# Attention as a stream of heads, with split decays, in a hybrid decoder step on one Trainium2 core

## What is computed

```python
def stick_breaking(q, k, v, q_pos0, sb_bias):
    ...
        mask = k_pos[None, :] < q_pos[:, None]
        z = jnp.einsum('bqhd,bkhd->bhqk', qb, kb).astype(jnp.float32) * scale + bias
        log_1m = jnp.where(mask, jax.nn.log_sigmoid(-z), 0.0)
        log_w = jax.nn.log_sigmoid(z) + lax.cumsum(log_1m, axis=3, reverse=True) - log_1m
        w = jnp.where(mask, jnp.exp(log_w), 0.0)
        outs.append(jnp.einsum('bhqk,bkhd->bqhd', w.astype(vb.dtype), vb))
```

## Time and profile before

| | |
|---|---|
| three runs | 2433.86, 2426.59, 2428.55 us; median 2428.55 |
| the profiled execution | 2428.46 us, span 2426.8 us, granted clock 0.998 |
| PE busy | 2382.4 us (98%), PEld 2183.8 (90%) |
| DVE, ACT, POOL busy | 1241.0 (51%), 994.5 (41%), 114.9 (5%) |
| traffic | 417.10 MB in 122660 packets, 23387 of them under 512 B |

### The profile page before, as it was taken

The page is one execution under the profiler, slowest core; times in us unless marked ns, Lnnn a source line. Parts: engine busy times, 40 slices in busy tenths (PEclk is TensorE's granted clock), DMA queues, the critical chain, the costliest instruction groups (busy, mean ns, idle before and its releaser), DMA issues.

```text
span 2426.8 us, 43808 instructions
## 1 busy us (share of the span) xinstructions
PE 2382.4 (98%) x18802; PEld 2183.8 (90%) x18802; DVE 1241.0 (51%) x1725; ACT 994.5 (41%) x1399; POOL 114.9 (5%) x232
## 2 busy tenths in 40 slices
PE   6999999999999999999999999999999999999998
PEld 5999999965699999999999999887777999999998
DVE  5533246755576333357523347755554758633245
ACT  5422235635456222346422245533223546522243
POOL 0000000122100000000000000012222100000000
PEclk9999999999999999999999999999999999999999
DMA  8555345785537653565754255544545456642254
GB/s 308 180 183 183 124 149 179 252 211 139 190 113 228 215 173 95 188 206 175 261 184 156 83 168 189 188 153 165 170 165 165 136 177 182 206 126 88 87 179 155
DMA packets 122660, 417.10 MB, mean 172 GB/s; under 512 B 23387, under 2 KB 27611, under 8 KB 122211
## 3 DMA queue, kind: packets, MB, share of 16 engines
q1 hardware_dynamic: 88962, 301.92, 39.1%
q10 hardware_dynamic: 18144, 62.03, 7.1%
q0 software_dynamic: 15360, 50.34, 6.3%
HBM read 390.84 MB, written 23.41 MB: 171 GB/s over the span
## 4 chain that ended last, share of the span: by engine, by line
PE 88%; DVE 5%; ACT 3%; DMA 2%; issue 1%; SPq 0%; ACTq 0%; POOL 0%; DVEq 0%; POOLq 0%
PE PS L2026 70%; PE PS L1425 3%; PE PS L1960 2%; DVE WL L2318 2%; PE PS L1990 2%; PE PS L1355 1%; ACT WH L2140 1%; DMA AFIRST<-in_w_ada 1%; PE PS L791 1%; PE PS L1309 1%; PE PS L1340 1%; PE PS L1350 1%; PE PS L753 1%; DMA RAW<-in_w_out 1%; PE PS L1321 1%
## 5 line engine op out<-in xcount | busy, mean ns | idle before, releaser
L2318 DVE TENSOR_TENSOR WL<-RAW,WH 128x1024 fp32r<-128x1024 f32 (+1 forms) x478 | 633.0, 1325 | 647.9 <-ACT WH L2140 647.2
L2026 PE MATMUL PS<-HH,WH 128*128 128x260 f32 x3432 | 796.6, 285 | 3.2 <-DVE QKVS L1119 1.8
L2026 PE MATMUL PS<-HH,WL 128*128 128x260 f32 x3432 | 786.5, 283 | 0.0
L2026 PE MATMUL PS<-HL,WH 128*128 128x260 f32 x3368 | 769.6, 283 | 0.0
L2140 ACT ACTIVATE WH<-RAW 128x1024 fp32r<-128x1024 f32 (+1 forms) x478 | 542.2, 1135 | 425.4 <-PE PS L2026 267.0
L2026 PEld LDWEIGHTS PS<-HH,WH 128*128 128x128 f32 x3432 | 569.9, 188 | 25.4 <-issue 16.8
L2026 PEld LDWEIGHTS PS<-HH,WL 128*128 128x128 f32 x3432 | 569.4, 188 | 0.0
L2026 PEld LDWEIGHTS PS<-HL,WH 128*128 128x128 f32 x3368 | 557.0, 188 | 0.6 <-issue 0.2
L2026 PE MATMUL PS<-GH,WH 128*128 128x260 f32 x1408 | 386.4, 285 | 0.9 <-DVE WL L2318 0.8
L2026 PE MATMUL PS<-GL,WH 128*128 128x260 f32 x1408 | 384.2, 283 | 0.0
L2026 PE MATMUL PS<-GH,WL 128*128 128x260 f32 x1408 | 383.5, 283 | 0.0
(11 more groups left out here) (340 smaller groups left out, 2317.5 us busy)
## 6 DMA issues: line engine op xcount, KB each, us to landing
RAW<-in_w_in SPq DMA_DIRECT2D x236, 512.0 KB, 3.7
RAW<-in_w_out SPq DMA_DIRECT2D x120, 704.0 KB, 4.0
AW<-in_w_ada ACTq DMA_DIRECT2D x114, 512.0 KB, 5.5
RAW<-in_w_odd SPq DMA_DIRECT2D x60, 512.0 KB, 3.7
RAW<-in_w_odout SPq DMA_DIRECT2D x30, 512.0 KB, 3.9
RAW<-in_w_even SPq DMA_DIRECT2D x28, 512.0 KB, 4.0
KV<-in_v_pages POOLq DMA_DIRECT2D x32, 256.0 KB, 4.8
SR<-in_ret_past POOLq DMA_DIRECT2D x32, 256.0 KB, 4.0
```

The costliest lines, as they stand in the source:

```text
L2026: last = nc.tensor.matmul(ps[:, x, 0:HT], w[:, k * P:(k + 1) * P], src[k0 + k][:, x, :], start=(begin and t == 0), stop=(end and t == 2))
L2318: nc.vector.tensor_tensor(low_, RAW[:, from_:from_ + w], high_.bitcast(F32), ALU.subtract).then_inc(lo_done, 1)
```

## The change

- **The stream of heads.** The loop runs over single heads. In head h block i: `sums(h, i)`, then `scores(h+3, i)` alone, then for even h > 0 a quarter of `values(h/2 - 1)`, and in heads 0, 3, 5 and 7 a quarter of `values_past`. The scores of head 1 and `sums_past` move into units 26 and 27; those of head 2 stand between unit 27 and the loop.
- **Split decays.** The softplus of a head is split into an fp32r high part (`high_part`, ACT, L918) and low part (`low_part`, DVE, L1105), 1280 columns each, and the sums become 20 fp32r matmuls per head (L810) in place of ten float32 ones, with fp32r copies of the triangle and of ones.
- **|z|** is taken by DVE for heads 0 to 2 and by ACT for heads 3 to 7 (`decay`). `Z` has four places and the decays five; `log_weights` now writes into the decay's place.
- **Rows of 16.** The host pads `pool_past` to 16 values, `US` is loaded and stored as a whole, and the host drops the first value of each row. The small loads are reordered. DVE waits for these loads (`ev_in`) at unit 0 of `evin`, and for the four stores (`pool_out`) before it writes `Z` of head 1; ACT waits for the stores too, before `high_part(0)`.

The core of the diff:

```diff
+        ZQ = [at(n, [CAUSAL], o)[:] for n, o in zip(("ZA", "ZB", "ZC", "ZD"), (sq_at, up_at, low_at, free_at))]
+        HOME_OF = (0, 1, 2, 3, 4, 0, 2, 3)
...
+                    for dst, src in ((US[:], pool_past), (PT[0:1, :], table), (PWT[:], pool_w), (RCP[:], pool_r),
+                                     (PSC[:], pool_s), (BIAS[:], bias_b)):
...
-                                     (pool_p, UP[:, :, SEQ + 1:SEQ + 16]), (pool_n, US[:, :, :, 1:16])):
-                        sp.dma_start(dst, src).then_inc(out_done, 16)
+                                     (pool_p, UP[:, :, SEQ + 1:SEQ + 16]), (pool_n, US[:])):
+                        sp.dma_start(dst, src).then_inc(pool_out, 16)
...
+            POOLED_AT = {(23, 4): 0, (24, 2): 1, (24, 4): 2, (25, 2): 3}
+            SCORES_AT = {(25, 3): 0, (25, 4): 1, (26, 1): 2, (26, 2): 3, (26, 3): 4, (26, 4): 5}
...
+                if (i, quarter) == (27, 3):
+                    sums_past()
...
+                pe.wait_ge(vp_evac, 2) if 4 * h + j < 10 else pe.wait_ge(z_dve, 4 * h + j - 1)
+                score(h, j, PS[0][:, j % 2, 0:LEN[j]]).then_inc(z_done, 1)
...
             def sums(h, i):
                 if i == 0:
-                    pe.wait_ge(sp_done, h + 1)
+                    pe.wait_ge(spl_done, h + 1)
...
+                for j in range(i, 4):
+                    w = TRIR if j == i else ONESR
+                    for x, part in enumerate((SPH[h % 2], SPL[h])):
+                        last = nc.tensor.matmul(PS[1][:, i % 2, (j - i) * P:LEN[i]], w[:],
+                                                part[:, OFF[j]:OFF[j] + LEN[j]], start=(j == i and x == 0),
+                                                stop=(j == 3 and x == 1))
...
+            PAST_AT = {0: 0, 3: 1, 5: 2, 7: 3}
+            for h in range(HEADS):
                 for i in range(4):
+                    sums(h, i)
+                    scores(h + 3, i)
+                    if h % 2 == 0 and h:
+                        values(h // 2 - 1, i)
+                    if h in PAST_AT:
+                        values_past(PAST_AT[h], i)
...
+                ada_step("head", h)
...
+            def high_part(h):
+                act.wait_ge(sp_done, h + 1)
+                if h == 0:
+                    act.wait_ge(pool_out, 64)
+                after(act, s_done, 4 * (h - 2) + 4)
+                nc.scalar.activation(SPH[h % 2], SP[h], ACT.Copy).then_inc(sph_done, 1)
...
+            for b in range(1, PAIRS):
+                if b > 1:
+                    outputs(b - 2)
+                decay(2 * b)
+                decay(2 * b + 1)
+                table(LOG_SET)
+                log(2 * b)
+                log(2 * b + 1)
+                high_part(2 * b)
+                table(EXP_SET)
+                weights(2 * b - 2)
+                weights(2 * b - 1)
+                high_part(2 * b + 1)
...
+            def low_part(h):
+                dve.wait_ge(sph_done, h + 1)
+                nc.vector.tensor_tensor(SPL[h], SP[h], SPH[h % 2].bitcast(F32), ALU.subtract).then_inc(spl_done, 1)
...
+            for h in range(HEADS):
+                if h == 4:
                     copy_past(0)
+                if h == 5:
                     copy_turned(0)
+                if h:
+                    low_part(h)
+                for i in range(4):
+                    log_weights(h, i)
+                    scored(h + 3, i)
+                if h in (3, 5):
+                    low((h - 3) // 2)
+                if h % 2:
+                    softplus(h + 1)
+                    softplus(h + 2)
+                ada_evac("head", h)
```

More of the change, by code:

```diff
@@ L786, in sums @@
             def sums(h, i):
                 if i == 0:
-                    pe.wait_ge(sp_done, h + 1)
+                    pe.wait_ge(spl_done, h + 1)
+                if h + i == 0:
+                    pe.wait_ge(const_ok, 3)
                 n = 4 * h + i
                 pe.wait_ge(lw_done, n - 1) if n >= 2 else pe.wait_ge(vp_evac, 4)
-                last = nc.tensor.matmul(PS[1][:, i % 2, 0:LEN[i]], TRI[:], SP[h % 4][:, OFF[i]:OFF[i] + LEN[i]],
-                                        start=True, stop=(i == 3))
@@ L814, in even_pe @@
-            sums_past()
-            scores_of_one()
-            ada_step("start", 0)
-            for t in range(PAIRS):
-                scores(t + 1, 0)
-                sums(2 * t, 0)
-                scores(t + 1, 1)
-                if t:
-                    values(t - 1)
-                sums(2 * t, 1)
-                scores(t + 1, 2)
-                sums(2 * t, 2)
-                if t == 2:
-                    gather(0)
-                scores(t + 1, 3)
-                sums(2 * t, 3)
-                if t < 3:
-                    values_past(t)
-                ada_step("head", 2 * t)
-                for i in range(4):
-                    sums(2 * t + 1, i)
-                if t == 3:
-                    values_past(3)
-                ada_step("head", 2 * t + 1)
+                for j in range(i, 4):
[4 more added lines that the diff above has]
+                                                stop=(j == 3 and x == 1))
@@ new lines, in sums, with values @@
+                last.then_inc(s_done, 1)
+            def values(t, i):
+                if i == 0:
+                    pe.wait_ge(w_done, 2 * t + 2)
+                    if t == 0:
+                        pe.wait_ge(zn_dve, 4)
+                    elif t == 1:
+                        pe.wait_ge(pool_low, 5)
+                    else:
+                        pe.wait_ge(ol_ready, t - 1)
+                for e in range(2):
+                    c = t * P + HD * e
+                    last = nc.tensor.matmul(PS[2][HD * e:HD * e + HD, t % 2, i * P:SEQ], VP[:, i, c:c + HD],
+                                            SP[2 * t + e][:, OFF[i]:OFF[i] + LEN[i]], start=(i == 0),
+                                            stop=(i == 3), tile_position=(0, HD * e))
+                if i == 3:
+                    last.then_inc(o_done, 1)
@@ L838, in even_pe @@
             gather(1)
-            values(3)
+            for i in range(4):
+                values(3, i)
             def chunk_ready(k):
@@ new lines, in even_dve @@
+            nc.vector.memset(PS[3][:, 1, :], 0.0).then_inc(z_zero, 1)
+            scored(2, 2)
+            scored(2, 3)
+            softplus(1)
+            sized(2)
+            for h in range(HEADS):
+                if h == 4:
+                    copy_past(0)
+                if h == 5:
+                    copy_turned(0)
+                if h:
+                    low_part(h)
+                for i in range(4):
+                    log_weights(h, i)
[6 more added lines that the diff above has]
+                ada_evac("head", h)
@@ L1203, in even_dve @@
+            low(2)
             copy_past(1)
```

360 lines of the change are left out of this document (162 added, 198 removed).

## The result

| | before | after |
|---|---|---|
| median of the runs, us | 2431.2 (2426.6 to 2435.3, 4 runs) | 2461.7 (2451.9 to 2466.0, 4 runs) |
| ratio, 95% interval | | 1.0120 (1.0098 to 1.0142) |
| profiled execution: time, span | 2428.46, 2426.8 | 2465.95, 2464.3 |
| mean granted clock of its span | 0.998 | 0.983 |
| last pooling matmul to first matmul of the projection | 536.51 to 654.19 = 117.7 | 536.75 to 691.97 = 155.2 |

The change is slower by 30 us where 11.5 was forecast. All of it lies in the attention: in the two profiles the stretch in the last but one row is 37.5 us longer, and so is the span. Each kernel has one profiled execution; its stretch, busy times and clock are of that one, and the medians are of all executions.

What follows compares the result with a forecast made beforehand. PE's work plus its gaps was taken to bound the kernel. Work -2.5 and gaps +14.4 gave +11.9, the stepping +11.0; with +11.5 taken, 2428.46 became 2440.0 us, range 2427 to 2450.

Steps and rivals of the forecast that it cites:

- The gaps: PE's waits in the attention, mostly for DVE between heads: 20.3 us against 5.9 before, +14.4 us.
- the stepping: Second count, walking the four instruction lists from unit 25: projection starts at 665.2 against 654.2, +11.0 us.
- The stops themselves: PE's waits ahead of heads 2, 3, 4, 5, 6, 7: 3.8, 2.1, 5.1, 0.8, 3.4, 0.6 us; before the last values 1.9.
- The 0.7 for late pages: PE's wait in head 7 for cached values, released one light head earlier: 0.7 us.
- Sums, -14.4: Split fp32r sums on PE, 3.14 us a head: eight heads 25.1 us instead of 39.5.
- All PE work, -2.5: PE's work in the attention: sums -14.4, scores +8.8, moved scores and past sums +0.3, quartered values +2.8 us.
- Lone scores, +8.8: Scores of heads 2 to 7 on PE: six single heads 17.7 us instead of three pairs 8.9.
- The rows of 16, nothing: Padded pooling rows, their transfers and new waits: nothing to 1 us.
- Cheap switches and narrow matmuls: Rival, 15%: 128-column fp32r matmuls at 0.06 us and free switches on PE; about 2432 us, no change.
- Overlapping scores: Rival, 5%: a lone 64-row score block overlaps the next sum at half its price; 8.5 us less, 2431.
- slow fp32r: Rival, 9%: fp32r matmuls of 256 and 128 columns at twice the assumed price; 10 us more, 2450.
- Covered gaps: Rival, 13%: DVE gaps between heads 1-2, 3-4, 5-6, 12.3 us, vanish; 2428, or 2420 with half the cheap prices.

Runs made afterwards that it cites:

- e11_stream_fill: e10_stream with three spare float32 matmuls (2.7 us) in PE's wait ahead of head 6: 2434.8 us.
- e6_spare: Changed kernel with each single score block of heads 3 to 7 joined by a spare partner block, each score also waiting for the previous block's evacuation: 2452.8 us.
- e12_control: Changed kernel with the additional evacuation waits of e6_spare but without its spare partner blocks: 2465.5 us.
- e1_fill: Changed kernel with 12 spare float32 matmuls in PE's waits ahead of heads 2, 3, 4 and 6: 2446.9 us.
- a0_again: The changed kernel run once more, unaltered, with a second profile: 2461.2 us.
- e3_f32: Changed kernel with the split of the sums undone (float32 sums, no high or low part), order and lone scores kept: 2443.4 us.
- b3_unpair: Kernel before with only the scores unpaired: each second head's block stands behind the sums of its block row: 2448.8 us.
- b1_rows: Kernel before with only the pooling rows of 16, loaded in the new order, and DVE's wait at unit 0: 2429.5 us.
- e2_order: Changed kernel with only DVE's order of softplus and low-part calls altered: 2434.2 us.
- e10_stream: Changed kernel with each pair's first logarithm early on ACT, DVE's softplus and low parts reordered, softplus of head 6 behind head 5's second block: 2434.4 us.
- b4_unpair_gap: b3_unpair with eight spare DVE passes ahead of the softplus of head 2, for a long PE stop there: 2455.7 us.
- e7_f32_gap: e3_f32 with four spare DVE passes (2.9 us) ahead of the softplus of head 2: 2448.4 us.

## Why the prediction was wrong

Time and range were missed (2440, up to 2450, against 2461.7); slower was forecast and is what came.

- **The step that failed** is the heading "The gaps": it priced each stop of PE at its length. The stop ahead of head 2 also lowered the clock, and with it the price of every PE instruction of the next 51 to 65 us. No rival had this, although the clock column stood in the earlier trace rows. The Trainium skill's page "TensorE: Matmul & The Clock Gate", section "HAM oscillation — how this bites in real kernels", describes a kernel whose waits between bursts of matmuls bring the clock to the low level; the traces agree (0.50 behind stops of 3.2 to 5.0 us) but for one stop of 3.31 us in e11_stream_fill, with 1.00 throughout, and the prediction cited the page for another sentence only. The stretch was put at 117.7 + 11 = 128.7 by the stepping; it is 155.2 with 72 us at the low clock, 149.5 with 54, 130.5 with 3. The first two differ by 5.8 us for 17 us of low clock, 0.34 for each, near the 0.32 of the eight times. That it is not half fits the rows: the waits inside the stay are not doubled (1.95 us ahead of head 3 at either clock), and the one ahead of head 4 is shorter at the low clock, 3.89 against 5.0.
- **The stops themselves** were right: 3.8, 2.1, 5.1, 0.8, 3.4, 0.6, 1.9 and 0.8 for the weights were forecast; measured 3.81, 1.95, 3.89 (4.99 in e6_spare, 5.00 in e12_control, where the clock was up ahead of it), none to 0.68, 3.38, 0.41, 1.72 and 0.73 (e1_fill). The 0.7 for late pages did not show, and in units 25 to 27 PE stood for 0.6, not 1.1. All stops together were put at 20.3 us; the idle time of the stretch is 15.8 in the profile of after and 17.2 in a0_again, 18.3 with 5.0 ahead of head 4, so the count was some 2 us too high.
- **Sums, -14.4:** a little too much. One head's split sums take 1.42 + 0.96 + 0.60 + 0.37 = 3.35 us where they stand in e11_stream_fill (from the start of each block to the next kind), 3.14 forecast; float32 blocks behind switches take 5.12 in e3_f32, 5.1 forecast. Eight times 3.35 is 26.8, against the forecast's 39.5 for the old sums -12.7. (e3_f32 and e11_stream_fill differ in PE's busy time by 124.47 - 110.05 = 14.4, the same number as the term but another difference: in e3_f32 all eight heads stand behind switches, before only four.) The 128-column matmul that had no row starts 0.06 us before its neighbour, not 0.107, and the switch behind it costs more: 0.20 from the last one to the next kind.
- **All PE work, -2.5:** measured -1.75 at the high clock. The same sum with float32 sums, +11.9, is 12.7 in e3_f32.
- **Lone scores, +8.8:** the second head of a pair is free, as read from the earlier trace rows, and the blocks took 1.05, 0.84, 0.63 and 0.42. In b3_unpair, another order, 3.6 us of waits came on top, and 5.6 that I put down to the low clock.
- **The rows of 16, nothing:** right, within 0.1% (b1_rows).
- **Cheap switches and narrow matmuls:** half came, 0.06 for 128 columns; the switches did not become free. **Overlapping scores, slow fp32r:** neither came. **Covered gaps:** not in this kernel; e2_order and e10_stream show what it needed, an order of DVE's calls.
- Without the low clock the time would have been some 2 to 3 us above the forecast, inside the stated range: 2442.5 on the line drawn through the changed kernel's own times (an estimate), 2442.8 in the better executions of e1_fill, which still have some low clock. That it comes so near is in part luck: 0.75 us too little work and some 2 us too much waiting stand against each other, and the rest of the difference has no row.

## What to carry over

Where a change makes TensorE wait longer at one place than it has so far, read the granted clock in a profile of the change before any other column, and give the low clock a rival with its own price in the forecast. A long sequence on another engine that PE waits for (here three passes of VectorE) is worth reordering even where that engine is half idle: moving four calls gave back 27 us, most of it through the clock. And two matmuls on half the array each are free as a pair, so an order that separates them must earn more than the second one's whole price.

## What the runs showed of the hardware that was not expected

- Stops of 3.81, 4.96, 3.78, 3.86 and 3.18 us each went with a fall to the low clock; it fell while PE still stood (0.68 in 593 to 594, PE back at 594.26). One of 3.31 us in e11_stream_fill did not: the clock reads 1.00 in 636 to 640, with PE busy 0.69 of 4.00 us, and behind it. Of the shorter ones, 1.94 us in e6_spare (0.59 in 612 to 616) and 2.49 in b4_unpair_gap were followed by it; 1.99 and 1.29 in e2_order, 2.69 in e7_f32_gap and 1.49 in before were not. In b3_unpair it fell among stops under 1 us with lone scores between. Length alone does not tell.
- The clock can stay at 1.2 GHz with PE busy throughout: 650 to 655 us in the kernel after, PE busy 5.00 of 5.00. Three stays measured 38 to 65 us; all others were of 3, 7 or 10.
- Useless matmuls in a stop are worth their place where they end ahead of what PE waits for (e1_fill), and useless blocks on an idle half of the array can be too (e6_spare against e12_control, 13 us).
